# Feature-major projections in 256-column jobs: six products per k tile read in turn, or four read in order

## The reference, cut to what matters

```
x = x + even_layer(x, ...)      # chunked attention and an mLSTM
x = x + odd_layer(x, ...)       # short convolutions, a gated LRU, a gated delta rule
x = x + ...                     # two more layers with rotary attention, then a final norm

proj = rmsnorm(x, norm_g) @ w_in          # 256 x 2048 times 2048 x up to ~9200
qa, ka, va, za, qb, kb, ... = split_cols(proj, EV_SIZES)
...
return y @ w_out
```

## Time and profile before

| | |
|---|---|
| median of 3 runs | 1827.17 us (1827.17 to 1827.51) |
| the profiled execution | 1827.51 us, its span 1825.6 us |
| PE busy | 1810.9 us, 99% of the span |
| PEld busy | 1677.6 us, 92% |
| DVE busy | 1151.8 us, 63% |
| ACT busy | 1009.0 us, 55% |
| POOL busy | 167.4 us, 9% |
| read from device memory | 336 MB |

### The profile page before, as it was taken

The page is one execution under the profiler, slowest core; times in us unless marked ns, Lnnn a source line. Parts: engine busy times, 40 slices in busy tenths (PEclk is TensorE's granted clock), DMA queues, the critical chain, the costliest instruction groups (busy, mean ns, idle before and its releaser), DMA issues.

```text
span 1825.6 us, 29960 instructions
## 1 busy us (share of the span) xinstructions
PE 1810.9 (99%) x12254; PEld 1677.6 (92%) x12254; DVE 1151.8 (63%) x1649; ACT 1009.0 (55%) x1580; POOL 167.4 (9%) x142
## 2 busy tenths in 40 slices
PE   9999999999999999999999999999999999999998
PEld 7999888888899999898889999888888999988887
DVE  6545655555666897687656677645565666755554
ACT  7435556764557765775553345566454344446644
POOL 0000000110011111101001111000000111100110
PEclk9999999999999999999999999999999999999999
DMA  9657555555555545455566555655565555565564
GB/s 367 191 171 222 187 167 194 179 173 191 189 186 169 167 151 161 160 175 162 189 209 197 196 184 172 200 178 169 186 195 197 196 194 176 172 195 178 171 207 139
DMA packets 96055, 340.48 MB, mean 187 GB/s; under 512 B 10816, under 2 KB 11456, under 8 KB 95792
## 3 DMA queue, kind: packets, MB, share of 16 engines
q1 hardware_dynamic: 94544, 333.91, 56.2%
q0 software_dynamic: 944, 3.61, 0.6%
q10 hardware_dynamic: 432, 1.06, 0.1%
HBM read 336.44 MB, written 2.10 MB: 185 GB/s over the span
## 4 chain that ended last, share of the span: by engine, by line
PE 88%; DVE 6%; ACT 3%; issue 1%; DMA 1%; POOL 0%; SPq 0%; ACTq 0%; POOLq 0%
PE ACC L764 17%; PE ACC L766 17%; PE ACC L765 17%; PE ACC L771 10%; PE ACC L773 10%; PE ACC L772 10%; DVE WL L1488 3%; ACT WH L1116 1%; DVE S L1736 1%; DMA RAW<-in_w 1%; PE PM L870 1%; PE PM L885 1%; PE PM L923 1%; PE PM L907 1%; PE PM L908 1%
## 5 line engine op out<-in xcount | busy, mean ns | idle before, releaser
L1488 DVE TENSOR_TENSOR WL<-RAW,WH 128x1024 fp32r<-128x1024 f32 (+2 forms) x632 | 779.3, 1244 | 530.6 <-ACT WH L1116 529.2
L1116 ACT ACTIVATE WH<-RAW 128x1024 fp32r<-128x1024 f32 (+3 forms) x633 | 650.0, 1040 | 459.2 <-PE ACC L766 227.6
L771 PE MATMUL ACC<-XHL,WH 128*128 128x256 f32 x1920 | 535.0, 279 | 2.2 <-DVE S L1509 2.2
L773 PE MATMUL ACC<-XHL,WL 128*128 128x256 f32 x1920 | 528.8, 275 | 0.0
L772 PE MATMUL ACC<-XHL,WH 128*128 128x256 f32 x1920 | 528.7, 275 | 0.0
L764 PE MATMUL ACC<-WH,XHL 128*128 128x512 f32 (+1 forms) x1044 | 396.9, 380 | 0.4 <-DVE WL L1488 0.4
L765 PE MATMUL ACC<-WL,XHL 128*128 128x512 f32 (+1 forms) x1044 | 389.0, 373 | 0.0
L766 PE MATMUL ACC<-WH,XHL 128*128 128x512 f32 (+1 forms) x1044 | 389.0, 373 | 0.0
L771 PEld LDWEIGHTS ACC<-XHL,WH 128*128 128x128 f32 x1920 | 369.3, 192 | 3.8 <-DVE WL L1488 2.5
L772 PEld LDWEIGHTS ACC<-XHL,WH 128*128 128x128 f32 x1920 | 369.3, 192 | 0.7
L773 PEld LDWEIGHTS ACC<-XHL,WL 128*128 128x128 f32 x1920 | 369.3, 192 | 0.0
(11 more groups left out here) (364 smaller groups left out, 1623.7 us busy)
## 6 DMA issues: line engine op xcount, KB each, us to landing
RAW<-in_w SPq DMA_DIRECT2D x605, 512.0 KB, 3.3
RAW<-in_wv SPq DMA_DIRECT2D x24, 344.0 KB, 3.1
X<-in_x SPq DMA_DIRECT2D x4, 512.0 KB, 12.3
RAW<-in_w SPq DMA_DIRECT2D x6, 256.0 KB, 5.0
Y<-in_xT SPq DMA_DIRECT2D x2, 512.0 KB, 10.5
S<-in_bias POOLq DMA_DIRECT2D x8, 128.0 KB, 2.5
S<-in_od_gate_w POOLq DMA_DIRECT2D x1, 1024.0 KB, 6.2
S<-in_final_norm POOLq DMA_DIRECT2D x1, 1024.0 KB, 7.8
```

The lines of the kernel that those rows point to most:

```text
L771: e.matmul(o, wh, pairs[:, 0], start=f and g % 2 == 0, stop=False, skip_group_check=True)
L773: m = e.matmul(o, wl, pairs[:, 0], start=False, stop=l, skip_group_check=True)
L1116: e.activation(hi, src, ACT.Copy).then_inc(s_hi)
L1488: e.tensor_tensor(lo, src, hi.bitcast(F32), ALU.subtract).then_inc(s_lo)
```

## The change

The 256-column feature-major jobs get the mode "wide". Per k tile they had six products of 256 moving columns; they get four. The high weight part of each group of 128 features now meets `xh` and `xl` in one product of 512 moving columns, and the two halves of the result go to separate 256-column regions of PSUM; the low weight part meets `xh` in a product of 256 columns and is added to the first region. A group's result is thus the sum of two regions, and the job fills both banks of its accumulator, where it filled one. DVE adds the regions at the read-out with a reduction over two (`halves_of`): a new instruction ahead of the row scaling in "feat" and ahead of the rotation in "rope", and in place of the copy in "sum". Behind it stands a wait of DVE on its own result.

Besides, `pairs` is gone: all feature-major products, wide or not, read their moving operand in plain order, and read-outs use no `by_token` and `tiles`. Token-major jobs keep reading in turn.

```
-EVAC = {"feat": (0, 1), ..., "rope": (0, 3)}
+EVAC = {"feat": (0, 2), ..., "rope": (0, 4)}
...
-            jobs.append(Job(layer, name, i, w, c0 + 256 * i, 256, "tile", kind, (0, 1, 2, 3)))
+            jobs.append(Job(layer, name, i, w, c0 + 256 * i, 256, "wide", kind, (0, 1, 2, 3)))
...
+        def halves_of(j):
+            return ACC[j % 2][:, :].rearrange("p (g h c) -> p g c h", g=2, h=2)
...
-                        pairs = XHL3[:, kt, :].rearrange("p (h t c) -> p h c t", h=2, t=2)
...
+                    elif J.mode == "wide":
+                        (wh0, wh1), (wl0, wl1) = ((w[:, kk, 0:128], w[:, kk, 128:256]) for w in (hi, lo))
+                        e.matmul(acc[0], wh0, XHL3[:, kt, :], start=f, stop=False, skip_group_check=True)
+                        e.matmul(acc[0][:, 0:256], wl0, xh, start=False, stop=l, skip_group_check=True)
+                        e.matmul(acc[1][:, 0:256], wl1, xh, start=f, stop=False, skip_group_check=True)
+                        m = e.matmul(acc[1], wh1, XHL3[:, kt, :], start=False, stop=l, skip_group_check=True)
                     else:
                         for g in range(w // 128):
...
-                            e.matmul(o, wh, pairs[:, 0], start=f and g % 2 == 0, stop=False, skip_group_check=True)
-                            e.matmul(o, wh, pairs[:, 1], start=False, stop=False, skip_group_check=True)
-                            m = e.matmul(o, wl, pairs[:, 0], start=False, stop=l, skip_group_check=True)
+                            e.matmul(o, wh, xh, start=f and g % 2 == 0, stop=False, skip_group_check=True)
+                            e.matmul(o, wh, xl, start=False, stop=False, skip_group_check=True)
+                            m = e.matmul(o, wl, xh, start=False, stop=l, skip_group_check=True)
...
-                        e.activation(tiles(conv_ring(k, i)), by_token(acc[i]), ACT.Copy).then_inc(s_evA)
+                        e.activation(conv_ring(k, i), acc[i], ACT.Copy).then_inc(s_evA)
...   # feat
+                    e.tensor_reduce(f, halves_of(j), AX, ALU.add).then_inc(s_evD)
                     e.wait_ge(s_row, 1)
+                    e.wait_ge(s_evD, D_AT[j] - 1)
+                    e.tensor_tensor(f, f, row2, ALU.mult).then_inc(s_evD)
...   # sum
-                    e.tensor_copy(tiles(conv_ring(c, i)), by_token(acc[0])).then_inc(s_evD)
+                    e.tensor_reduce(two(conv_ring(c, i)), halves_of(j), AX, ALU.add).then_inc(s_evD)
...   # rope
+                    e.tensor_reduce(dst, halves_of(j), AX, ALU.add).then_inc(s_evD)
...
+                    e.wait_ge(s_evD, D_AT[j] - 3)
                     for x, y in ((lo, hi), (hi, lo)):
-                        e.tensor_tensor(t2[x], src[y], sin[y], ALU.mult).then_inc(s_evD)
-                    e.tensor_tensor(dst, src, cos, ALU.mult).then_inc(s_evD)
+                        e.tensor_tensor(t2[x], dst[y], sin[y], ALU.mult).then_inc(s_evD)
+                    e.wait_ge(s_evD, D_AT[j] - 1)
+                    e.tensor_tensor(dst, dst, cos, ALU.mult).then_inc(s_evD)
```

## The result

The changed kernel takes 1854.4 us (1853.1 to 1855.6) where the kernel before takes 1827.3: the ratio is 1.0146, 95% interval 1.0129 to 1.0164. Slower by 1.5%, 27 us; 1849 was forecast. The profiled execution took 1853.35 us, its span 1851.5. Runs of one kernel differ by about 2 us: the three runs of the changed kernel whose granted PE clock was 0.999 of full speed over the span had spans of 1851.0 to 1851.5 us, the two at 0.998 1853.2 and 1853.4.

The account below looks back on a forecast made before the run. PE was taken as the bound, busy 99% of the span, through distances between product starts. Plain order +14.9 and +5.1 us plus DVE +2.1 gave +22.1, so 1849 us; range 1816 to 1890.

Parts of the forecast that it names:

- The distances in turn: 256-column jobs: 512-column products 216 ns apart, 256-column ones 111.4; a k tile 654.8 ns instead of 668.4.
- Plain order costs: Feature-major products on PE: plain order slows the stream by 6%, a k tile to 689.6 ns; +14.9 and +5.1 us.
- s: Time lost per 256 columns read in plain order on PE: 6.5 ns chosen, within bounds 0 and 109.
- the maximum of stream and load: 256-column products on PE: distance is the longer of load, 111.4 ns, and plain stream, 109.3 + s.
- Rival 1: Feature-major products on PE: plain order is free, 1820 us; chance 0.28.
- rival 2: Feature-major products on PE: plain order takes two cycles per column, 2438 us; chance 0.02.
- Rival 3: Rotary jobs: plain order free, but DVE's 2.4 us reductions remove its lead, 1829 us; chance 0.09 together with Rival 4.
- Rival 4: Whole kernel: s between 1.5 and 3.1 ns, parts cancel, within 4 us of 1827; chance 0.09 together with Rival 3.
- DVE's price: Read-outs of the 256-column jobs: 1.2 us per reduction, +55 us of DVE work in all.
- `xcs`: Layer 1 stage: no PE gain counted, four DVE read-outs of +0.5 us on the path, +2.1 us.
- What hides DVE's work: Rotary and layer 0 jobs: longer read-outs hidden, next splits five pieces ahead, accumulator wanted back a whole job later.
- The figure of 614 GB/s: PE's moving-operand path: were plain reading held to this skill-page rate, 512 columns would take 427 ns, which is rival 2.

Follow-up runs that it names:

- merge only: Changed kernel with its merged products and two-region sums kept, but every feature-major moving operand read in turn: 1818.3 us, ratio 0.9954 to the kernel before.
- order only: Kernel before with its six products per k tile kept, but all feature-major products and the 16-column job in plain order: 1870.7 us, ratio 1.0241.
- idle reductions: Kernel before plus two unread 512-element DVE reductions ahead of the read-out of each of the 48 256-column jobs: 1832.2 us, ratio 1.0030.
- small program: Not the layers: rows of 32 products per form, no other engine at work; its last plain loads stand 112 ns apart, then 213 at clock 0.50.

## Why the prediction came out right, step by step

**The distances in turn** (216 and 111.4 ns, 654.8 per k tile if the order cost nothing): right, 655 ns in merge only.

**Plain order costs.** Right in sign and nearly in size, but the size was a choice within wide bounds, so that the nearness is in part luck. With s = 6.5 ns per 256 columns a k tile was to take 689.6 ns; it took 89.2/128 = 697. The excess lies in the 512-column products, which took 233 ns where 229 were reckoned, so that s was about 8; the 256-column ones between them took 115 to 116, as reckoned. The narrow products, one behind the other, took 120 where 115.8 were reckoned. There the weak step was the maximum of stream and load: with a short load the plain product takes 114 ns and loads alone stand 112 apart, so the maximum would be 114, and it takes 120. The two add up in part. Instead of +14.9 and +5.1 us the terms were +18.9 (layer 0, `qds` and `kds`, the rotary jobs) and +9.4.

**Rival 1** (free) falls with order only, **rival 2** (two cycles per column) with the same run: +8%, not +100%. Most of the doubling in the earlier trace rows thus goes with the type; plain float32 read in turn was not tried. **Rival 3** (DVE late in the rotary jobs) falls with the idle reductions and with merge only: no stage of these jobs waits, with DVE at 77 to 84% in the changed kernel. **Rival 4** (s between 1.5 and 3.1 ns) falls with the measured 8.

**DVE's price.** The reduction was put at 1.2 us and took 1.22. The sum was put at +55 us and came to +64.5. The 48 reductions take 58.7 us in place of 5.5 us of copies; 14.7 us more lie in the splits, whose mean went from 1261 to 1291 ns. With the idle reductions the splits take 1288 ns as well, so this goes with DVE's added work and not with the order.

**`xcs`** was to pay 2.1 us for DVE and became 1.5 shorter. This step failed. PE's wait there shrank instead of growing, and the clock did not fall. The prediction read the clock as at the upper level all through, from a line of 40 slices; its own have 0.97 in this stretch, and 3.4 us at the lower level are worth 1.6 us. The work added to DVE alone costs at most 0.3 us there besides such a stretch. With the 1.0 us that the output stage gave back, the shorter `xcs` offset part of the larger loss on PE (28.3 us where 20.0 were forecast), and so 22 us forecast came near to 26 of span. That is luck: two errors of opposite sign.

**What hides DVE's work** was said to be an accumulator wanted back a whole job later. The 16-column job is the exception, as the idle reductions show.

**The figure of 614 GB/s.** By the 614 GB/s that the Trainium skill's "SBUF — State Buffer" (section "A bandwidth-pool intuition that's wrong (but worth ruling out)") gives for 2-byte elements, plain order would have taken 427 ns per 512 columns. It takes 227 to 237, over 1100 GB/s. The same page of the Trainium skill has a penalty for each step to a new 16-byte line, and full bandwidth from two hits in a line on. The first has the sign wrong for reading in turn of 4-byte elements (216 ns against 227 to 237 in plain order). By the second every second column, two of the four in a line, would be at the full rate; it takes 453 ns, nearly as much as every fourth column with 461.

## What to carry to other kernels

Where PE is the bound, read its time as distances between starts, and keep the order in which the moving operand is read apart from the form of the product: here a merge worth 0.5% came together with an order that cost 2.0% (2.4% with the six products). For fp32r operands read in turn from two places an even number of columns apart, four or more, starting at column 0 of the run (or, as in these kernels, at a multiple of 256); for bf16 read in plain order. A DVE cost is hidden as long as the job that follows is long; look for the one short job. And before a few microseconds in one stage are put down to a wait, compare the granted clock of that stage: one stretch of 3.4 us at the lower level is 1.6 us here, as much as the waits in question.

## What was not expected of the hardware

Every second fp32r column costs 453 ns for 512 where every column, in turn from two places, costs 216; bf16 read in turn costs 485 ns where plain costs 216. Every second bf16 column costs nothing (113 ns for 256). The granted clock fell to 1.2 GHz for 3.4 us within layer 1 in all profiled kernels but the changed one, twice with the idle reductions, and PE was busy all through the 3 us ahead in some of these cases. In the small program it doubled the distance of plain loads, 112 to 213 ns, which hides whether a load from every second column costs anything at the upper level.
